# A two-layer hybrid decoder: out, down and value products with activations stationary and the residual kept with tokens on partitions

## What is computed

```python
def rmsnorm(x, g):
    return x * rsqrt(mean(x * x, axis=-1) + 1e-6) * g

# layer 0: SSD and Conformer mixer, layer 1: short convolution and sparse attention
proj = rmsnorm(x, mix_norm) @ w_in          # 2048 -> about 7k or 8k columns
x = x + concat(mixer outputs) @ w_out       # 3072 -> 2048
u = causal_dwconv(rmsnorm(x, ffn_norm) @ w_up, conv_w, conv_b)   # 2048 -> 2 * 5632
g, v = split(u)
x = x + (silu(g) * v) @ w_down              # 5632 -> 2048
# after both layers
out = rmsnorm(x, final_norm)
```

## Time and profile before

| | us |
|---|---|
| median of 3 runs | 2696.22 |
| lowest, highest | 2696.09, 2702.37 |
| the profiled execution | 2700.2 |
| its span, first to last instruction | 2698.5 |
| PE busy in it | 2643.3 (98%) |
| DVE, ACT, POOL busy | 1837.8, 1396.6, 148.6 |
| mean granted TensorE clock | 0.990 |

### The profile page before, as it was taken

How to read it: one execution, slowest core, us unless ns; L and a number is a source line. 1 busy time by engine, 2 the same in 40 slices (tenths; PEclk the granted TensorE clock), 3 DMA queues, 4 the chain that set the end, 5 groups by cost and what they waited for, 6 DMA issues and landing times.

```text
span 2698.5 us, 42752 instructions
## 1 busy us (share of the span) xinstructions
PE 2643.3 (98%) x16064; PEld 2331.0 (86%) x16064; DVE 1837.8 (68%) x2630; ACT 1396.6 (52%) x1882; POOL 148.6 (6%) x150
## 2 busy tenths in 40 slices
PE   7999999999999999999999999899999999999999
PEld 7999898888888888888788888778888888888887
DVE  4699867667765776577765667656677657765775
ACT  5588665446644553454443544553465535543553
POOL 0001100210000000002200000002200000000003
PEclk9999999999999999999998999999999999999999
DMA  6454335555555555554755665115555555555544
GB/s 210 160 177 153 112 122 162 181 191 187 187 187 187 188 188 191 191 190 163 207 170 159 185 188 184 48 36 187 195 179 190 182 187 190 190 190 191 187 164 148
DMA packets 238535, 464.49 MB, mean 172 GB/s; under 512 B 12506, under 2 KB 14170, under 8 KB 238426
## 3 DMA queue, kind: packets, MB, share of 16 engines
q1 hardware_dynamic: 236922, 460.73, 51.5%
q10 hardware_dynamic: 1504, 2.29, 0.3%
HBM read 460.90 MB, written 2.10 MB: 172 GB/s over the span
## 4 chain that ended last, share of the span: by engine, by line
PE 90%; DMA 3%; DVE 3%; ACT 2%; issue 1%; SPq 0%; DVEq 0%; ACTq 0%
PE bank L1725 48%; PE bank L1728 24%; PE bank L1971 4%; PE bank L1973 4%; PE bank L1972 4%; DVE weight_tail L1089 1%; ACT weight_head L606 1%; PE bank L2053 1%; DMA weight_raw<-in_ffn_w_up 1%; PE bank L2007 1%; PE bank L2088 1%; DMA w<-in_nsa_cmp_w 1%; DMA weight_raw<-in_cd_w_in 1%; PE bank L1911 1%; DMA weight_raw<-in_ffn_w_down 0%
## 5 line engine op out<-in xcount | busy, mean ns | idle before, releaser
L1089 DVE TENSOR_TENSOR weight_tail<-weight_raw,weight_head 128x2048 fp32r<-128x2048 f32 (+1 forms) x456 | 999.9, 2193 | 758.7 <-ACT weight_head L606 757.1
L606 ACT ACTIVATE weight_head<-weight_raw 128x2048 fp32r<-128x2048 f32 (+1 forms) x456 | 832.2, 1825 | 969.5 <-DMA weight_raw<-in_ffn_w_up 314.0
L1725 PE MATMUL bank<-norm_in,weight_head 128*128 128x512 f32 x3840 | 1212.4, 397 | 11.2 <-DVE residual L1445 6.6
L1728 PEld LDWEIGHTS bank<-norm_in,weight_tail 128*128 128x128 f32 x3840 | 724.6, 189 | 171.8
L1728 PE MATMUL bank<-norm_in,weight_tail 128*128 128x256 f32 x3840 | 757.1, 279 | 0.0
L1725 PE MATMUL bank<-mixed,weight_head 128*128 128x512 f32 x2176 | 702.3, 397 | 7.0 <-DVE mixed L1506 3.7
L1725 PEld LDWEIGHTS bank<-norm_in,weight_head 128*128 128x128 f32 x3840 | 587.3, 189 | 13.0 <-DVE weight_tail L1089 7.5
L1728 PEld LDWEIGHTS bank<-mixed,weight_tail 128*128 128x128 f32 x2176 | 410.8, 189 | 80.5
L1728 PE MATMUL bank<-mixed,weight_tail 128*128 128x256 f32 x2176 | 463.0, 280 | 0.0
L1725 PEld LDWEIGHTS bank<-mixed,weight_head 128*128 128x128 f32 x2176 | 347.7, 189 | 27.1 <-DVE residual L1445 5.7
L1971 PE MATMUL bank<-norm_in,weight_head 128*128 128x256 f32 x896 | 260.7, 291 | 6.8 <-ACT zx L856 4.4
(11 more groups left out here) (290 smaller groups left out, 1549.3 us busy)
## 6 DMA issues: line engine op xcount, KB each, us to landing
weight_raw<-in_ffn_w_up SPq DMA_DIRECT2D x176, 1024.0 KB, 4.9
weight_raw<-in_ffn_w_down SPq DMA_DIRECT2D x64, 1024.0 KB, 5.0
weight_raw<-in_cd_w_in SPq DMA_DIRECT2D x64, 1024.0 KB, 5.7
weight_raw<-in_ab_w_in SPq DMA_DIRECT2D x56, 1024.0 KB, 5.0
weight_raw<-in_ab_w_out SPq DMA_DIRECT2D x32, 768.0 KB, 4.3
weight_raw<-in_ffn_w_down SPq DMA_DIRECT2D x32, 768.0 KB, 4.2
weight_raw<-in_cd_w_out SPq DMA_DIRECT2D x32, 768.0 KB, 4.2
x_stage<-in_x SPq DMA_DIRECT2D x4, 512.0 KB, 5.9
```

The source lines that it names most:

```text
L606: act.activation(WHEAD[:, off % RING, 0:kt * CW], WRAW[:, off % RING, 0:kt * CW], ACT.Copy)\
L1089: dve.tensor_tensor(WTAIL[:, off % RING, 0:kt * CW], WRAW[:, off % RING, 0:kt * CW], WHEAD[:, off % RING, 0:kt * CW].bitcast(F32), ALU.sub ...
L1725: pe.matmul(bank[c][:, :], head, rhs[:, u * s.kt + k, :], start=u == 0 and k == 0, stop=False)
L1728: mm = pe.matmul(bank[c][:, 0:SEQ], tail, rhs[:, u * s.kt + k, 0:SEQ], start=False, stop=u == s.units - 1 and k == s.kt - 1)
```

## The change

1. `H` is kept as 2 tiles of 128 tokens by 2048 channels. The input lands in it directly; `turn_residual` and its copies are gone, and so are the transposes of the result.
2. Out and down products, and in1's two value groups, are computed by `row_group`: a 128x128 piece of `Y` (or `U`) is stationary and 512 weight columns move. For each 128 tokens (`t`) and each `k` there are three matmuls of 512 columns, into one bank.
3. Groups of out and down alternate between banks 0, 1 and banks 2, 3. The table of what a group waits for becomes an argument (`free`); after such a product the next one waits for nothing at its first two tiles.
4. DVE adds a bank to `H` in one step of 128x512 (`row_add`).
5. ACT squares `H` with a sum over the free axis (`row_squares`); POOL's statistics and PE's sum over ones are gone. The factor is worked out on 128x2 and spread to 128x256 by two matmuls (`norm_behind`), then copied (`factors_copied`).
6. For the norms behind out0, down02 and out1 PE turns `H` back, eight transposes behind the first unit of the next group (`turn_rows`), and ACT and DVE write `U` from the banks.
7. Value groups are evicted by ACT straight with tokens on partitions (`v_rows`); the 16 value transposes are gone.
8. At the end POOL multiplies by the gain (loaded as a broadcast of 1 MB by SP before layer 1's MLP), ACT and DVE scale by the factor and store.

```diff
+FREE_BELOW, FREE_AFTER_ROWS, FREE_AFTER_V = (-3, -2, -1, 0), (-4, -4, -2, 0), (-2, 0, 0, 0)
-        H = take("residual", [P, DT, SEQ], F32)
+        H = take("residual", [P, NT, D], F32)
...
+            def row_group(s, i, lhs, banks, free, ready=None, after=None):
...
+                    for t in range(NT):
+                        if u == 0:
+                            pe.wait_ge(bank_read, tile + free[t])
+                        dst = bank[banks[t]][:, :]
+                        for k in range(s.kt):
+                            cols = slice(k * CW, (k + 1) * CW)
+                            head, tail = WHEAD[:, u % RING, cols], WTAIL[:, u % RING, cols]
+                            row = u * s.kt + k
+                            x_h, x_t = lhs[:, row, t * P:(t + 1) * P], lhs[:, row, SEQ + t * P:SEQ + (t + 1) * P]
+                            pe.matmul(dst, x_h, head, start=u == 0 and k == 0, stop=False)
+                            pe.matmul(dst, x_h, tail, start=False, stop=False)
+                            mm = pe.matmul(dst, x_t, head, start=False, stop=u == s.units - 1 and k == s.kt - 1)
+                            if k >= s.kt - 2:
+                                mm.then_inc(cols_done, 1)
...
+            def row_product(name, lhs, ready=None, norm=None, after=None):
...
+                        row_group(s, i, lhs, (0, 1), (-3, -2), ready, after)
+                    else:
+                        row_group(s, i, lhs, (2 * (i % 2), 2 * (i % 2) + 1), (-5, -4),
+                                  after=turn_behind(norm, s, i - 1) if norm is not None else None)
...
+            def turn_rows(n, s, i):
+
+                pe.wait_ge(bank_read, s.tile + 4 * i + 4)
+                pe.wait_ge(u_ready, DT * n + 4 * (i - 1) if i >= 2 else DT * n)
+                pe.wait_ge(rstd_copied, n - 1)
+                for k in range(2):
+                    for j in range(2):
+                        for t in range(NT):
+                            tile = 4 * i + 2 * k + j
+                            tr = pe.transpose(bank[4 + 2 * (i % 2) + k][:, (2 * j + t) * P:(2 * j + t + 1) * P],
+                                              H[:, t, tile * P:(tile + 1) * P], IDENT[:, :])
+                    tr.then_inc(h_turned, 1)
...
+            def norm_behind(n, s):
+
+                def go(u):
+                    if u == 0:
+                        turn_rows(n, s, 3)
+                    if u == 2:
+                        pe.wait_ge(rstd_ready, n)
+                        pe.wait_ge(u_ready, DT * n + 12)
+                        for t in range(NT):
+                            mm = pe.matmul(bank[5][:, t * P:(t + 1) * P], RTOK[:, t:t + 1].to_broadcast([P, P]), IDENT[:, :],
+                                           start=True, stop=True)
+                        mm.then_inc(rstd_spread, 1)
...
+            def row_add(s, e, i, t):
+
+                dve.wait_ge(cols_done, e * 4 - 4 + 2 * (t + 1))
+                h = H[:, t, i * CW:(i + 1) * CW]
+                dve.tensor_tensor(h, bank[2 * (i % 2) + t][:, :], h, ALU.add).then_inc(bank_read, 2)
...
             def root(n):
 
                 act.wait_ge(var_ready, n)
-                act.activation(ROOT, RSTD[:, :], ACT.Sqrt).then_inc(root_ready, 1)
-
-                act.wait_ge(rstd_ready, n)
+                act.activation(RSQ, RVAR, ACT.Sqrt).then_inc(root_ready, 1)
...
+            def v_rows(q, e):
...
+                    act.activation(ZX[:, j:j + 4, SEQ + t * P:SEQ + (t + 1) * P],
+                                   bank[t][:, :].rearrange("p (g d) -> p g d", g=KVH), ACT.Copy, scale=RTOK[:, t:t + 1])\
+                       .then_inc(bank_read, 2)
...
+            sp.wait_ge(y_ready, 5 + 2 + NSA_HEADS)
+            sp.dma_start(FG[:, :], final_norm.rearrange("(a n) -> a n", a=1).to_broadcast([P, D])).then_inc(fg_landed, 16)
             load_mlp(1)
```

More of the change, by code:

```diff
@@ L1460, in residual_groups @@
-            def residual_groups(name, n, gain, uready):
-                s = SPANS[name]
-                kts = ahead(s.unit + s.units, s.units, n)
-                with dve.Fori(0, n) as i:
-                    residual_group(i * 4 + s.tile, i * 4 + HALVES[name], i * s.units + (s.unit + s.units), i, gain,
-                                   i * 4 + uready, kts)
+                    if k == 1 and gain is not None:
+                        turned_tails(norm, i, gain)
+                        if i == 3:
+                            norm_factor(norm)
@@ L1718, in product_group @@
                     for c in range(4):
[L1719 to L1720 removed]
+                        if u == 0:
+                            pe.wait_ge(bank_read, tile + free[c])
                         for first_k in range(0, s.kt, 2):
```

409 lines of the change are left out of this document (189 added, 220 removed).

## The result

The changed kernel takes **2668.75 us** (median of 4 runs, 2664.89 to 2670.54) against 2696.15 of the kernel before (4 runs, 2691.8 to 2702.37): the ratio is 0.9895, 95% interval 0.9872 to 0.9917, or 27.4 us less. The forecast was 2681.5 with a range of 2655 to 2706 and "faster" at 0.68. Direction and range held; the middle was 12.8 us too high. The profiled execution took 2668.58 us with a span of 2666.9, so between the two profiled executions it is 31.6 us.

A forecast was written before the change was run, and what follows sets the result against it. PE, busy for 98% of the span, was taken as the bound. Terms 0 - 9.0 - 4.6 - 5.1 + 5.0 - 1.0 = -14.7 us took the profiled 2700.2 to 2685.5, or 2681.5 against the median 2696.2; range 2655 to 2706.

The forecast's parts named there:

- The products with Y: Out and down products: 3264 matmuls of 512 columns at 0.2335 us, 762 us against 761.6 before; change 0.
- that rival: Fixed cost per instruction: loss per matmul is loading weights, so fewer loads pay; 2681.5 - 18 = 2664 us, chance 0.24.
- The triple's pace: Row matmuls go like in0's triples, 0.24 us per 512 columns; 2705 us, slower, chance 0.15.
- bare columns: Row matmuls cost nothing on top of their columns, 0.2133 us per 512; 2611 us, chance 0.04.
- The value groups: In1's two value groups: 192 matmuls of 512 for 128 patterns of 512 + 256, 44.8 for 44.8 us; 0.
- Transposes and sums: On PE: old transposes and sums over ones go, 96 transposes and six small matmuls come, nothing hides them; +5.0 us.
- The waits for the residual: PE's waits for DVE's additions to the residual all go, as the next product finds free banks; -9.0 us.
- The turns in the groups: Rival: waits move to twelve turns or bank 3; 2700 us, chance 0.10; 44 us more if all wait, 0.05.
- The first group behind a norm: PE's wait there goes, since ACT no longer waits for the factor and its arithmetic is on 128x2; -4.6 us.
- Half clock: Three stretches of 3.4 us at clock 0.50 behind PE's waits go, 1.7 us each; -5.1 us.
- Behind the last product: The end of the run: a DVE and ACT chain of 11.8 us replaces 12.8; -1.0 us, bounds -3 and +2.
- At nothing: Priced at zero: DVE's shorter additions, squares swapped between ACT and POOL, the gain's broadcast (+3 if it does not fit).

The follow-up runs named there:

- the long chain: The changed kernel with the norm's factor arithmetic back at 128x256 and ACT waiting for the factor, started at the new, earlier place: 2659.57 us.
- same banks: The changed kernel with all groups of out and down in banks 0 and 1: 2686.46 us.
- late factor: The changed kernel with the norm's factor arithmetic at 128x256, ACT's wait for it, and its old, late place: 2676.93 us.

## Why the prediction was right in sign and too small in size

**The products with Y: 0 forecast, -22 measured.** This is the step that failed. "I take 0.2335 ... I stay with the row that has the right width": 3264 x 0.2335 = 762. The measured 0.2266 gives 740. The stages bear the difference out: a clean down stage lost 2.1 us (89.2 to 87.1, 0.697 per pattern of 1536 columns before), and out1 some 5.0, from 135.8 without its waits (0.707 per pattern: units of three row tiles break the pairs into two and one) to 130.8 without its new transposes. The 0.70 stands between the two. The 0.235 in the earlier trace rows was the distance between starts inside a mixed pattern, where most of the time on top of the columns falls behind the 512s and less behind the 256s (0.233 and 0.231 against 0.115 and 0.119). Only the sum of a pattern is a cost; how it splits inside says where the starts fall. The bound that was worked out beside it, the sum shared by instructions, gave 0.2283 and -17, and was nearly right; the rest is that it took 15 ns from the pattern where a triple pays 13.3, which the earlier trace rows already showed: 0.12 - 256/2400. Two rows agreed on a fixed cost, and I set that rival at 0.24. Its reason, that fewer loads pay, is not shown: half the load's width bought nothing at 512 columns, and the narrow pieces at 256 leave the load's part open. What is shown is a cost per matmul instruction.

**The triple's pace, 0.24, and bare columns, 0.2133:** both wrong. In0's triple has no pace of its own; its 0.12 is the same 13.3 ns at half the width. The Trainium skill ("TensorE: Matmul & The Clock Gate", Back-to-back issue gap), cited ahead of the run, gives about 216 ns by its formula N / 2.4 + 2.5; the trace has 226.6. It has the right shape, a constant beside the columns, and for this format too small a constant: 13.3 where it has 2.5.

**The value groups: 0 forecast.** 192 x 0.2266 = 43.5 against 44.8: -1.3.

**Transposes and sums: +5.0 forecast.** The timeline has eight transposes at 557.75 and the next product matmul at 558.54, 0.79 us later:

```profile
557.75 1.04 PE L1788 MATMUL bank<-ident,residual 128*128 128x128 f32 x8
558.54 0.70 PE L1722 MATMUL bank<-norm_in,weight_head 128*128 128x512 f32 x2
```

Twice the transposes cost 0.109 us each. The rate, the number and "nothing hides them" hold.

**The waits for the residual: -9.0 forecast, -6.1 measured.** The mechanism is right and shown by the kernel without the alternation. "Late next is bank 3, with about 1.5 us in hand" was checked against DVE's tail alone, not against what that tail waits for: in in1 the weight's DMA put the additions 4 us late and bank 2 was the one that waited. The turns in the groups, which I had feared in a rival, did not wait.

**The first group behind a norm: -4.6, as forecast, in the main for another reason.** In up00 and up10 the earlier place is enough, with the long chain and ACT's wait as well; in in1 the long chain brought 1.2 of 2.3 us back at the earlier place, so there both count. In up00 DVE starts the reciprocal at 563.06 (0.15 us now against 1.75 at 577.39 in the earlier trace rows), some 10 us before the first bank is read:

```profile
563.06 0.15 DVE L1088 RECIPROCAL small<-small 128x2 f32<-128x2 f32 x1
...
573.66 0.42 DVE L1107 COPY rstd<-bank 128x256 f32<-128x256 f32 x1
```

**Half clock: -5.1 forecast.** The three stretches are gone. Elsewhere in0 has one of 3.4 instead of 6.8, and the one in attention 10.2 instead of 6.8, which cancel. The experiments agree: waits put back brought stretches back (same banks, late factor).

**Behind the last product: -1.0 forecast, +1.0 measured** (13.8 us behind 2653.1 against 12.8). The timeline of the end, against the earlier trace rows:

```profile
2653.06 0.69 DVE L1426 TENSOR_TENSOR residual<-bank,residual 128x512 f32<-128x512 f32 x1 [0.21 <-PE bank L1763]
...
2654.53 1.28 ACT L1045 ACT_TABLE_LOAD   x1
...
2658.47 0.20 ACT L1045 ACTIVATE small<-small 128x1 f32<-128x1 f32 x1 [2.44 <-DVE small L1462]
2658.57 2.55 ACT L1052 ACTIVATE out_stage<-h_gained,small 128x512 f32<-128x512 f32 x4
```

The 2.55 us are four scalings on ACT in a row where I had counted two behind two others, and the store of 512 KB takes 3.8 us to landing against the 3.1 taken. It is inside the bounds of -3 and +2. The parts that the forecast lists for its 11.8 add up to 11.5.

**At nothing.** The gain's broadcast takes 6.6 us to landing and the up stage behind it is 0.5 us longer, 0.9 of wait in it, which went when the additions moved with the broadcast left where it was. The waits for hidden tiles stayed in down02 and down12 (4.2 us for 3.7), as said. Down10 has none, before or after; the forecast was wrong to name it. Its stage lost 4.2 us where its matmuls account for 2.1, because one of the nine waits for the residual stood there, between its first two groups (timeline of DVE and PE in the kernel before):

```profile
2142.18 2.29 DVE L1089 TENSOR_TENSOR weight_tail<-weight_raw,weight_head 128x2048 fp32r<-128x2048 f32 x1 [5.32 <-ACT weight_head L606]
...
2145.32 0.73 PE L1725 MATMUL bank<-mixed,weight_head 128*128 128x512 f32 x2 [1.21 <-DVE residual L1445]
```

DVE's additions are 2.0 us less per group, not 3.3, which is what they took in all before (107.4 us to 42.9 over 32 groups).

**The sum, between the profiled executions:** -22.0 - 1.3 + 5.0 - 10.7 (13.6 us of waits to 2.9) - 5.1 + 1.0 = -33.1, against -31.6 measured. Other waits of PE, which the forecast put at nothing, grew by 1.8: 0.9 for `conf_pad` in in0, 0.4 for `w` (2.3 to 2.7) and 0.5 for the hidden tiles (3.7 to 4.2). With them the sum is -31.3. Forecast was -14.7, and the difference is the first term, with errors of 3 and 2 us against it. Against the medians 4.2 us less is seen, because the profiled execution of the kernel before stood 4.0 above its median.

## What to carry to other kernels

Take the cost of a matmul from whole repeating patterns, written as columns over the clock plus a constant per instruction, and test it on two widths before you price a new one; the distance between two starts inside a mixed pattern is not a price. Here wide moving operands paid because there is a quarter fewer instructions for the same columns. Where an engine's queue is in order, put the work that another engine waits for (here additions and small tails) ahead of a step that may wait for a DMA, and start a chain as early as its inputs allow before you shorten it. Before a difference between two single executions is called chance, list what the engine waited for in both: here a wait for one DMA went with most of it.

## What the runs showed of the hardware

- An fp32r matmul with 128 stationary columns costs its columns at 2.4 GHz plus 13.3 ns, at 256 columns (0.120) and at 512 (0.2266), whether or not the same stationary operand comes twice in a row.
- With 64 stationary columns and 512 moving ones it costs 0.230, 3 ns more, although the busy time of a load falls from 0.187 to 0.134 us; with 32 and 256 it costs 0.113, 7 ns less than with 128. Not explained.
- Pairs of 512 and 256 columns, two and two, pay 14.1 ns per matmul, and four and four pay more (178.3 to 179.6 for a stage of 1024, 1.3 ns each). Not explained.
- The stretch at half clock behind the compression goes with the wait for one DMA in front of it: in fourteen profiles 13.7 or 17.1 us where the wait was 1.2 us or more, 10.2 where it was 0.7, none where it was 0.5 or absent, and without it in1 with attention was some 5 to 7 us shorter. A single execution cannot tell a gain of that size from nothing.
